# Mixer recurrence: second token block in reversed order, both blocks' level products joined per head, keys packed by ScalarE

## The reference, cut to what matters

```python
f = lb + (1.0 - lb) * sigmoid(f_logit)
k = 1.0 - f
# per head: S_t = diag(f_t) S_{t-1} + k_t^T i_t ;  o_t = S_t^T q_t
o = rmsnorm(o, g_norm) * silu(g)
# beside it, on u: trailing mean over 2/4/8/16 tokens minus the token, a linear map per group
```

## Time and profile before

| what | value |
|---|---|
| time before, median of 3 runs | 1795.06 us (1794.76 to 1795.96) |
| the profiled execution's own time | 1796.16 us |
| its span in the profile | 1794.4 us |
| mean granted TensorE clock of the core | 0.997 |

### The profile page before, as it was taken

How to read it: one execution, slowest core, us unless ns; L and a number is a source line. 1 busy time by engine, 2 the same in 40 slices (tenths; PEclk the granted TensorE clock), 3 DMA queues, 4 the chain that set the end, 5 groups by cost and what they waited for, 6 DMA issues and landing times.

```text
span 1794.4 us, 20287 instructions
## 1 busy us (share of the span) xinstructions
PE 1771.8 (99%) x8106; PEld 1470.4 (82%) x8106; DVE 1452.8 (81%) x1433; ACT 952.4 (53%) x1011; POOL 171.1 (10%) x193
## 2 busy tenths in 40 slices
PE   8999999999999999999999999999999999999998
PEld 7788888888888888888888887888888888888886
DVE  6999999999888777755755548999999999887776
ACT  4755555555555445743234446555655555565543
POOL 3011111111000000350000002011111111000000
PEclk9999999999999999999999999999999999999999
DMA  7566666666566665665454654666666666565664
GB/s 258 179 208 196 203 200 199 200 206 204 178 209 199 199 199 198 214 185 156 131 150 126 208 171 164 204 207 199 200 199 202 208 198 202 192 195 188 210 201 151
DMA packets 155774, 345.37 MB, mean 192 GB/s; under 512 B 10568, under 2 KB 11152, under 8 KB 155296
## 3 DMA queue, kind: packets, MB, share of 16 engines
q1 hardware_dynamic: 154832, 339.79, 60.4%
q0 software_dynamic: 736, 4.26, 0.7%
q10 hardware_dynamic: 112, 0.03, 0.0%
HBM read 341.94 MB, written 2.10 MB: 192 GB/s over the span
## 4 chain that ended last, share of the span: by engine, by line
PE 94%; DVE 2%; ACT 1%; DMA 1%; issue 1%; DVEq 0%; POOLq 0%; POOL 0%; SPq 0%; ACTq 0%
PE ps L1371 21%; PE ps L1373 21%; PE ps L1372 21%; PE ps L1569 7%; PE ps L1571 7%; PE ps L1570 7%; PE ps L1642 2%; PE ps L1639 2%; PE ps L1641 2%; PE ps L1742 1%; PE ps L1521 1%; DVE wlo L854 1%; DMA raw<-in_ffn_w_down_dram 1%; DVE x L1105 1%; ACT xT_hi L528 0%
## 5 line engine op out<-in xcount | busy, mean ns | idle before, releaser
L854 DVE TENSOR_TENSOR wlo<-raw,whi 128x1024 fp32r<-128x1024 f32 x440 | 545.6, 1262 | 165.0 <-ACT whi L468 162.5
L468 ACT ACTIVATE whi<-raw 128x1024 fp32r<-128x1024 f32 x440 | 457.6, 1056 | 311.4 <-DMA raw<-in_ffn_w_down_dram 155.7
L1371 PE MATMUL ps<-whi,xT_hi 128*128 128x512 f32 x1088 | 431.2, 396 | 8.5 <-DVE wlo L854 5.9
L1373 PE MATMUL ps<-whi,xT_lo 128*128 128x512 f32 x1088 | 425.4, 391 | 0.0
L1372 PE MATMUL ps<-wlo,xT_hi 128*128 128x512 f32 x1088 | 424.8, 390 | 0.0
L1371 PE MATMUL ps<-whi,hT_hi 128*128 128x512 f32 x672 | 262.4, 391 | 2.8 <-DVE wlo L854 2.8
L1373 PE MATMUL ps<-whi,hT_lo 128*128 128x512 f32 x672 | 261.5, 389 | 0.0
L1372 PE MATMUL ps<-wlo,hT_hi 128*128 128x512 f32 x672 | 261.5, 389 | 0.0
L1371 PEld LDWEIGHTS ps<-whi,xT_hi 128*128 128x128 f32 x1088 | 205.2, 189 | 53.5 <-issue 8.6
L1373 PEld LDWEIGHTS ps<-whi,xT_lo 128*128 128x128 f32 x1088 | 205.0, 188 | 43.6
L1372 PEld LDWEIGHTS ps<-wlo,xT_hi 128*128 128x128 f32 x1088 | 205.2, 189 | 40.8
(11 more groups left out here) (188 smaller groups left out, 2531.7 us busy)
## 6 DMA issues: line engine op xcount, KB each, us to landing
raw<-in_ffn_w_down_dram SPq DMA_DIRECT2D x136, 512.0 KB, 3.7
raw<-in_ffn_w_gate_dram SPq DMA_DIRECT2D x96, 512.0 KB, 3.8
raw<-in_ffn_w_up_dram SPq DMA_DIRECT2D x96, 512.0 KB, 3.7
raw<-in_w_in_dram SPq DMA_DIRECT2D x80, 512.0 KB, 3.7
srawB<-in_ffn_w_gate_dram SPq DMA_DIRECT2D x40, 512.0 KB, 4.8
srawB<-in_ffn_w_up_dram SPq DMA_DIRECT2D x40, 512.0 KB, 4.8
srawA<-in_ffn_w_gate_dram SPq DMA_DIRECT2D x40, 512.0 KB, 4.6
srawA<-in_ffn_w_up_dram SPq DMA_DIRECT2D x40, 512.0 KB, 4.6
```

Of the source, the lines that this page charges most:

```text
L468: nc.scalar.activation(whi[:, slot(g), :], raw[:, slot(g), :], ACT.Copy).then_inc(hi_ready, 1)
L854: V.tensor_tensor(wlo[:, slot(g), :], raw[:, slot(g), :], whi[:, slot(g), :].bitcast(f32), ALU.subtract).then_inc(lo_ready, 1)
L1371: mm(bank, a_hi, whi[:, s, c0:c0 + NT], start=start, stop=False, skip_group_check=skip)
L1373: return mm(bank, a_lo, whi[:, s, c0:c0 + NT], start=False, stop=stop, skip_group_check=skip)
```

## The change

Inside the mixer, tokens 128 to 255 are held in reversed order. A new permutation matrix `flip` (ones on the anti-diagonal) takes the place of `ident` when block 1 of x is transposed, in the band matrices of block 1, and when block 1 of the rows is transposed back. The sums of squares of block 1 go through one small product with `flip`. T, qP and kR are laid out [128, 2 blocks, 8 heads, 128]. With block 1 reversed, its later half of a group lies where the earlier half of block 0 lies. ScalarE packs the two earlier halves side by side into `kP` [128, 8, 128]; TensorE takes, per head, all of `kP` against the 64 later queries of both blocks, which is one product of 128x128 in place of two of 128x64. On VectorE the updates are split by block, done ahead of the masked copies, and the copies take four heads at a time.

The core of the diff:

```diff
-    T = at("T", 64, [P, HEADS, SEQ])
+    T = at("T", 64, [P, TOK, HEADS, P])
+    kP = at("kP", 116, [P, HEADS, P])
...
             load_gain(D1, g1post_d)
+            pool.wait_ge(vcol_tr, 1)
+            link(nc.gpsimd.memset(flip[:], 0.0))
+            nc.gpsimd.affine_select(out=flip[:], in_=flip[:], compare_op=ALU.not_equal, fill=1.0, base=1 - P,
+                                    pattern=[[1, P]], channel_multiplier=1).then_inc(flip_ok, 1)
             inv_root(2, 1, 0, 1)
...
+                if p >= 40 and (p - 40) % 3 == 0 and (p - 40) // 3 < len(LEVELS):
+                    li = (p - 40) // 3
+                    m = LEVELS[li]
+                    if li:
+                        act.wait_ge(k_ok, 2 * li)
+                    else:
+                        act.wait_ge(fk_ok, 2)
+                    for b in range(TOK):
+                        src, dst = (flat(t3).rearrange("p (g two m) -> p g two m", two=2, m=m) for t3 in (kR[:, b], kP[:]))
+                        nc.scalar.activation(dst[:, :, b, :], src[:, :, b, :], ACT.Copy).then_inc(kp_ok, 1)
...
                 for c in range(2):
-                    for q in range(4):
-                        h = 4 * c + q
-                        dst = S[:, h, 0:SEQ].rearrange("p (g two m) -> p g two m", two=2, m=m)[:, :, 1, :]
-                        msk = mask[:, li, :].rearrange("p (g m) -> p g m", m=m).bitcast(i32)
-                        V.copy_predicated(dst, msk, ps[6 + c][:, P * q:P * (q + 1)].rearrange("p (g m) -> p g m", m=m))
+                    found = ps[6 + c][:].rearrange("p (h b g m) -> p h b g m", h=4, b=TOK, m=m)
+                    for b in range(TOK):
+                        dst = S[:, 4 * c:4 * c + 4, b * P:(b + 1) * P].rearrange("p h (g two m) -> p h g two m", two=2, m=m)
+                        msk = mask[:, li, 64 * b:64 * b + 64].rearrange("p (g m) -> p g m", m=m).bitcast(i32)
+                        ins = V.copy_predicated(dst[:, :, :, 1 - b, :], msk.unsqueeze(1).broadcast_to([P, 4, 64 // m, m]),
+                                                found[:, :, b])
+                ins.then_inc(lev_ready, 1)
...
+                for b in range(TOK):
+                    early, late, end = order[b]
+                    k = pairs[b][1]
+                    V.tensor_tensor(k[:, :, early, :], k[:, :, early, :], whole(b, late), ALU.mult).then_inc(k_ok, 1)
+                for b in range(TOK):
+                    early, late, end = order[b]
+                    q = pairs[b][0]
+                    ins = V.tensor_tensor(q[:, :, late, :], q[:, :, late, :], whole(b, early), ALU.mult)
+                link(ins)
...
                 if p == 8:
-                    mean_square(2, x_sq, TOK * DN * 2)
+                    dve.wait_ge(turned_ok, 1)
+                    V.tensor_reduce(out=ms[:, 2, 0:1], in_=ss[:, 2, 0:1, :], op=ALU.add, axis=AX.X)
+                    link(V.tensor_reduce(out=ms[:, 2, 1:2], in_=ps[6][:, 0:DN], op=ALU.add, axis=AX.X))
...
                     li = (p - 40) // 3 - 1
+                    dve.wait_ge(lev_done, li + 2)
+                    next_level(li)
                     take_level(li)
-                    next_level(li)
-                    V.sem_inc(lev_ready, 1)
...
+                    pe.wait_ge(x_sq, TOK * DN * 2)
+                    mm(ps[6][:, 0:DN], flip[:], ss[:, 2, 1, :], start=True, stop=True).then_inc(turned_ok, 1)
...
                     pe.wait_ge(lev_ready, li + 1)
+                    pe.wait_ge(kp_ok, 2 * li + 2)
                     for hh in range(HEADS):
-                        for b in range(TOK):
-                            n = 2 * hh + b
-                            right = qP[:, hh, P * b:P * (b + 1)].rearrange("p (g two m) -> p g two m", two=2, m=m)
-                            ins = mm(ps[6 + n // 8][:, 64 * (n % 8):64 * (n % 8 + 1)].rearrange("p (g m) -> p g m", m=m),
-                                     kR[:, hh, P * b:P * (b + 1)], right[:, :, 1, :], start=True, stop=True)
+                        out = ps[6 + hh // 4][:, P * (hh % 4):P * (hh % 4 + 1)]
+                        ins = mm(out.rearrange("p (b g m) -> p b g m", b=TOK, m=m), kP[:, hh, :],
+                                 both_halves(qP, hh, m, 1, 0), start=True, stop=True)
```

More of the change, by code:

```diff
@@ L426, in _ @@
                     link(nc.gpsimd.memset(band[:, wi, t:t + 1], 1.0 / (t + 1)))
-                for c0, n in ((0, SEQ), (SEQ, P)):
+                for c0, n, first, step, one in ((0, SEQ, 0, 1, ident), (SEQ, P, P - 1, -1, flip)):
                     b = band[:, wi, c0:c0 + n]
[L429 to L433, removed]
+                    link(nc.gpsimd.affine_select(out=b, in_=b, compare_op=ALU.is_ge, fill=0.0, base=-first,
+                                                 pattern=[[1, n]], channel_multiplier=-step))
+                    link(nc.gpsimd.affine_select(out=b, in_=b, compare_op=ALU.is_ge, fill=0.0, base=first + w - 1,
+                                                 pattern=[[-1, n]], channel_multiplier=step))
+                    link(nc.gpsimd.tensor_tensor(b[:, 0:P], b[:, 0:P], one[:], ALU.subtract))
             for li, m in enumerate(LEVELS):
@@ L1248, in next_level @@
             def next_level(li):
                 m = LEVELS[li]
[L1252 to L1256, removed]
-                if li < len(LEVELS) - 1:
+                pairs = [[level_pairs(t4, b, m) for t4 in (qP, kR, T)] for b in range(TOK)]
@@ new lines, in next_level, with whole @@
+                order = [(0, 1, m - 1), (1, 0, 0)]
+                def whole(b, side):
+                    end = order[b][2]
+                    return pairs[b][2][:, :, side, end:end + 1].broadcast_to([P, 512 // m, m])
+                for b in range(TOK):
[6 more added lines that the diff above has]
+                    ins = V.tensor_tensor(q[:, :, late, :], q[:, :, late, :], whole(b, early), ALU.mult)
@@ L1258, in next_level @@
+                link(ins)
+                if li < len(LEVELS) - 1:
+                    for b in range(TOK):
+                        early, late, end = order[b]
+                        f = pairs[b][2]
+                        ins = V.tensor_tensor(f[:, :, late, end:end + 1], f[:, :, late, end:end + 1],
+                                              f[:, :, early, end:end + 1], ALU.mult)
                     link(ins)
-                    ins = V.tensor_tensor(f[:, :, 1, m - 1:m], f[:, :, 1, m - 1:m], f[:, :, 0, m - 1:m], ALU.mult)
@@ L1447, in transpose_unit @@
                     k = 4 * n + c
[L1448 removed]
+                    ins = nc.tensor.transpose(ps[TB[u % 3]][:, c * P:(c + 1) * P], x[:, t, k * P:(k + 1) * P],
+                                              (flip if step == 1 and t else ident)[:])
                 ins.then_inc(u_tr, 1)
@@ L1513, in keep_busy, with transpose_tile @@
                     nc.tensor.transpose(ps[JUNK][:, 0:P], ident[:], ident[:])
-            def transpose_tile(src, c0, banks, signal, each):
+            def transpose_tile(src, c0, banks, signal, each, second=ident):
                 for c in range(2):
```

58 lines of the change are left out of this document (36 added, 22 removed).

## The result

The changed kernel took 1781.35 us (median of 4 runs, 1780.48 to 1782.74) beside 1795.51 us for the kernel before: ratio 0.9921, 95% interval [0.9904, 0.9938]. Two later comparisons of the same two kernels gave 0.9927 [0.9914, 0.9939] and 0.9926 [0.9914, 0.9939], that is 11.8 and 13.1 us by their medians. So the question of this study is a small one: whether the mechanism was the forecast one, and where the missing 1 to 2 us belong.

What follows compares the result with a forecast made beforehand. TensorE was taken as the bound, busy 1771.8 of 1794.4 us and waiting for nothing over the levels. -12.2 + 0.25 = -11.9 us against the median of 1795.06 gave 1783.1 us, range 1781.8 to 1786.8.

Steps and rivals of the forecast that it cites:

- TensorE, the levels: Level products on TensorE: 1.78 us instead of 3.52 at each of seven levels, saving 1.74 each, 12.2 us in all.
- Strides: Strided moving operand of the new level product: slowdown between 1 and 2.04 times, taken as 1; otherwise 1.7 to 3.7 us.
- The norm: Small product with `flip` for the sums of squares: adds 0.25 us on TensorE (0.22 to 0.5), without a wait.
- packing: ScalarE's two copies of 512 elements per level: 1.2 us, 8.5 over all, hidden while TensorE is busy elsewhere.
- level work: VectorE's keys, queries, gates and masked copies per level: 6.8 us at the first, about 5.2 from m = 4 on.
- half 47: TensorE's p = 47, named VectorE's tightest place: it starts 1.8 us late, then needs 7.0 of 8.26 us.
- The cover: VectorE's spare time before TensorE's next level, 8.26 us after the last: 1.5 us at the first level.
- VectorE is late next: Once the saving comes, VectorE is the next engine to be late, with 1.2 us or more of room.
- A: Rival: slower TensorE at m = 1 and 2 (+1.7 to +3.7 us) or late VectorE (up to 1); 1784.8 to 1786.8; chance 0.10.
- B: Rival: no gain, the new product costs double or issues as two halves, level stays 3.5 us; 1795.3 us; chance 0.06.
- C: Rival: VectorE's masked copies at three times their cost bound the levels, 8.3 us lost; 1803.4 us; chance 0.04.

Runs made afterwards that it cites:

- the delay: Changed kernel with two idle 128x1024 operations per level on VectorE ahead of the masked copies: 1786.24 us, ratio 0.9956 to the kernel before.

## Why the prediction was right or wrong

**TensorE, the levels.** Right in its mechanism, its place and, to 0.05 us a level, its size: 1.74 forecast, 12.55 / 7 = 1.79 measured. The mis-sized term is the level's cost before. The forecast read it as 3.52 us and put the 0.28 of the matmul behind it among the unchanged 8.26 us of the halves, though it used that same 0.28 for the product with `flip`. With that matmul a level cost 3.80 us before and costs 2.01 now (2.05 at the first two).

**Strides.** Taken as 1.0 times, measured 1.02 at two levels. The upper end, +1.7 to +3.7 us, carried the whole upper half of the range and was not needed.

**The norm.** 0.25 us forecast, 0.23 measured, no wait.

**ScalarE and VectorE.** 1.2 us of packing per pair (1.28 as two of 0.641); 6.8 us of level work (6.3), 5.2 from the third level on (4.8); the start 1.8 us late behind half 47 (1.6). The cover held. That VectorE is late next was right; that half 47 is the tightest place was not: with the delay TensorE waited 0.73 and 1.66 us behind the first two levels and 0.22 behind half 47. The room was 1.8 us at both places, where 1.5 and 1.2 had been forecast.

**The rivals.** A is 0.08 us, B and C do not occur.

**The range.** This is what failed, by two steps. The first is the term above: by sum, the steps give 12.55 - 0.23 = 12.3 us against 11.9, which is 0.4 of the 1.75 us between the forecast of 1783.1 and the 1781.35 of the first comparison. The second is the lower side of the range. 1782.2 from all runs together lies inside 1781.8 to 1786.8, the first comparison's 1781.35 does not. The lower end came from the scatter of three runs of the kernel before (1794.76 to 1795.96), while single runs of it lie between 1792.4 and 1799.3, those of the changed kernel between 1779.7 and 1785.7, and the changed kernel's three medians are 1781.35, 1782.94 and 1782.40. A sum good to 0.4 us was given a lower side of 1.3 us, in a prediction that itself called effects below 3.6 us not to be told from none; and the lower side got no allowance for a term read too small. The rest of the 1.75 us goes with two runs of four at the highest clock, which by the table above is taken as chance.

## What to carry to other kernels

On this path a small f32 product costs 0.22 us, twice the step of 0.11, whether it has 16 columns or 128, so where two such products each use half of their weights, it pays to pack the used halves into one set of weights, even at the price of a permuted layout and of copies on an engine with idle time. Read such a group together with the matmul behind it, because a part of its cost is recorded there. Before a gap is called filled, look in the trace whether the filling runs in it. And take a range's width from many runs and their clocks, not from the spread of three.

## What the runs showed of the hardware that had not been expected

The cost of a group of eight products of up to 128 columns, with the next big matmul, is constant to 0.02 us (2.01 to 2.03), but the records move it: the narrower the group, the longer the next big matmul (0.34 us behind 16 columns, 0.23 behind 128). A moving operand of 4-byte elements is free at stride 2 (0.04 us of 1.78), costs 1.56 times at stride 3 and 1.95 to 2.10 times at 4 to 16. And one and the same program has a fall of TensorE's clock behind the same wait of 2.2 us in some executions and not in others, in both kernels (0.66 over 5 us in one profile of the kernel before and 1.00 in the other; 0.77 over 5 us in one of the changed kernel); the fall of 0.66 is worth 3.4 us at the lower level.
